# Seven block products for the second attention branch's queries, keys and values

## The reference, cut to what matters

```python
h = x @ w_in
qa, ka, va, qb, kb, vb = jnp.split(h, ...)
oa = windowed_gqa_sink(rope(qa), rope(ka), va, sink)
ob = neighborhood_attention(qb, kb, vb, rpb)
return jnp.concatenate([oa, ob], axis=-1) @ w_out
```

## Time and profile before

| | us |
|---|---|
| median of three runs (2304.95 to 2306.76) | 2305.78 |
| profiled execution, its own time | 2306.97 |
| its span | 2305.1 |
| TensorE busy in it (matmuls) | 2269.1 |
| VectorE, ScalarE, GpSimd busy | 979.0, 443.7, 73.8 |

### The profile page before, as it was taken

How to read it: one execution, slowest core, us unless ns; L and a number is a source line. 1 busy time by engine, 2 the same in 40 slices (tenths; PEclk the granted TensorE clock), 3 DMA queues, 4 the chain that set the end, 5 groups by cost and what they waited for, 6 DMA issues and landing times.

```text
span 2305.1 us, 25572 instructions
## 1 busy us (share of the span) xinstructions
PE 2269.1 (98%) x10790; PEld 1371.1 (59%) x10790; DVE 979.0 (42%) x1950; ACT 443.7 (19%) x1011; POOL 73.8 (3%) x130
## 2 busy tenths in 40 slices
PE   9999999999999999999999999999999999999998
PEld 6568547886487459997434433335999643333342
DVE  3567646667576557653211111125774311111122
ACT  3410003258110011220211211101132121111111
POOL 2000000000000000000000000000000000000000
PEclk9999999999999999999999999999999999999999
DMA  7279625354698415246999999995426599999997
GB/s 292 113 306 401 257 78 204 147 183 173 243 407 327 178 59 203 97 176 262 382 429 427 427 427 428 427 418 193 164 96 247 223 409 427 427 429 427 427 428 285
DMA packets 59168, 671.64 MB, mean 291 GB/s; under 512 B 7505, under 2 KB 7793, under 8 KB 18721
## 3 DMA queue, kind: packets, MB, share of 16 engines
q1 hardware_dynamic: 51888, 649.45, 69.1%
q0 software_dynamic: 7152, 20.43, 2.6%
HBM read 666.59 MB, written 3.26 MB: 291 GB/s over the span
## 4 chain that ended last, share of the span: by engine, by line
PE 87%; DMA 10%; DVE 3%; issue 0%; ACT 0%; SPq 0%; POOL 0%; DVEq 0%; POOLq 0%; ACTq 0%
PE ps L101 84%; DMA ring<-in_exp_w 8%; DVE arena L114 1%; PE ps L349 1%; DVE arena L117 1%; DMA arena<-ssm_rows 1%; PE ps L2753 1%; DMA ring<-in_ada_w 0%; PE ps L638 0%; DMA ring<-in_attn_w_in 0%; PE ps L1915 0%; DVE X L117 0%; PE ps L1234 0%; ACT arena L106 0%; DVE arena L110 0%
## 5 line engine op out<-in xcount | busy, mean ns | idle before, releaser
L101 PE MATMUL ps<-arena 128*64 128x512 f32 (+8 forms) x4036 | 954.6, 465 | 16.2 <-DMA arena<-in_exp_w 5.9
L101 PEld LDWEIGHTS ps<-arena 128*128 128x128 f32 (+2 forms) x4036 | 462.4, 167 | 464.5 <-issue 434.6
L101 PE MATMUL ps<-ring,arena 128*64 128x512 f32 (+2 forms) x1720 | 460.7, 584 | 3.2 <-DMA ring<-in_exp_w 3.2
L101 PE MATMUL ps<-XTGB,ring 128*128 128x256 f32 (+1 forms) x2160 | 423.5, 353 | 0.0
L101 PEld LDWEIGHTS ps<-XTGB,ring 128*128 128x128 f32 x2160 | 367.4, 191 | 52.5 <-issue 11.2
L101 PEld LDWEIGHTS ps<-ring,arena 128*64 128x64 f32 (+1 forms) x1720 | 174.9, 151 | 259.5 <-issue 253.9
L122 DVE COPY arena<-ps 128x512 f32<-128x512 f32 (+5 forms) x133 | 63.3, 496 | 417.4 <-PE ps L101 298.6
L121 ACT COPY arena<-ps 128x512 f32<-128x512 f32 (+3 forms) x179 | 81.5, 474 | 676.2 <-PE ps L2753 283.7
L101 PE MATMUL ps<-XTGB,arena 128*64 128x512 f32 (+2 forms) x736 | 200.7, 428 | 0.0
L105 ACT ACTIVATE arena<-ps 128x512 f32<-128x512 f32 (+2 forms) x95 | 51.2, 545 | 679.4 <-PE ps L101 674.6
L101 PE MATMUL ps<-ring,XTGB 128*128 128x512 f32 (+3 forms) x484 | 168.5, 503 | 2.9 <-DMA ring<-in_attn_w_in 2.7
(11 more groups left out here) (151 smaller groups left out, 949.8 us busy)
## 6 DMA issues: line engine op xcount, KB each, us to landing
arena<-in_exp_w SPq DMA_DIRECT2D x90, 2048.0 KB, 26.7
ring<-in_exp_w SPq DMA_DIRECT2D x68, 2048.0 KB, 27.9
ring<-in_mlp_w SPq DMA_DIRECT2D x25, 2048.0 KB, 8.8
ring<-in_ada_w SPq DMA_DIRECT2D x20, 2048.0 KB, 9.6
XTGB<-in_exp_w SPq DMA_DIRECT2D x18, 2048.0 KB, 32.3
ring<-in_ssm_w_in SPq DMA_DIRECT2D x12, 2048.0 KB, 7.6
ring<-in_w_in SPq DMA_DIRECT2D x12, 2048.0 KB, 7.8
ring<-in_gate_w SPq DMA_DIRECT2D x12, 2048.0 KB, 7.5
```

What stands on the lines that cost most here:

```text
L101: return self.e.matmul(o, lhsT=lhsT, rhs=rhs, start=start, stop=stop, skip_group_check=True)
```

## The change

q, k and v of the second branch are each made by seven block products. x's four block sums (`ab_x_sums`) are made once, on VectorE, after the first rope step. The weights' four block sums (`ab_sums`: three new blocks and one in place of a weight block, four instructions of 128x1024) are made on GpSimd for each of the three slabs. TensorE makes the products in four groups per slab (`ab_products`): group 0 the products 1 and 2 (added in PSUM), group 1 the products 6 and 5, group 2 the products 7 and 3, group 3 the product 4. For q and k a product is 2 x 4 matmuls over 128 columns, for v four over 256. ScalarE copies group 0's result (`ab_first`), VectorE adds the others (`ab_results`, seven adds per slab, after each pair's `normalise`). In the new `BETWEEN` the numbers 0 to 11 are 4 * slab + group, 12 to 15 are `out_a`, 16 is the first part of `out_b(0)`. The diff, cut to its core:

```diff
+        qX = [arena.get(4, P) for _ in range(4)]
+        qS = [[arena.get(4, T) for _ in range(2)] for _ in range(2)]
+        qS4 = arena.get(4, T)
-        BETWEEN = [((0,), (4,)), ((1,), (5,)), ((8,), ()), ((9,), ()), ((2,), (6,)), ((3,), (7,)), ((10,), (11,)),
-                   ((12,), (13,))]
+        BETWEEN = [((0,), (1,)), ((2,), (3,)), ((4,), (5,)), ((6,), (7, 8)), ((9,), (10,)), ((12,), (11,)),
+                   ((13,), (14,)), ((15,), (16,))]
+        AB_GROUPS = ((1, 2), (6, 5), (7, 3), (4,))
+
+        def ab_x_sums(v):
+            x1, x2, x3, x4 = qX
+            v.wait_ge(at("XT", 0, 0), at("XT", 0, 1))
+            k = v.then_inc(v.tt(x1, XT[:, 0:4, P:T], XT[:, 0:4, 0:P], ALU.subtract), "abX")
+            v.then_inc(v.tt(x3, XT[:, 4:8, P:T], XT[:, 0:4, P:T], ALU.subtract), "abX")
...
+        def ab_sums(e, k):
+            w = weights(f"ab{k}")
+            s1, s2 = qS[k % 2]
+            e.wait_ge(at("w", f"ab{k}"), at("abp", k - 2, 1) if k >= 2 else None)
+            i1 = e.then_inc(e.tt(s1, w[:, 0:4, T:2 * T], w[:, 4:8, T:2 * T], ALU.add), ("abS", k, 5))
+            e.wait_ge(i1)
+            i2 = e.then_inc(e.tt(s2, s1, w[:, 0:4, 0:T], ALU.subtract), ("abS", k, 6))
+            e.then_inc(e.tt(w[:, 0:4, T:2 * T], w[:, 0:4, 0:T], w[:, 0:4, T:2 * T], ALU.subtract), ("abS", k, 7))
+            e.wait_ge(i2, at("abp", k - 1, 2) if k else None)
+            e.then_inc(e.tt(qS4, w[:, 4:8, 0:T], s2, ALU.subtract), ("abS", k, 3))
...
+        def ab_products(pe, k, r):
...
+            ps = bank(pe, "abp", k, r, hold=r == 0)
+            pe.wait_ge(at("w", f"ab{k}"), at("abX"))
+            for n, p in enumerate(AB_GROUPS[r]):
+                x, y = pairs[p]
+                if p in (3, 5, 6, 7):
+                    pe.wait_ge(at("abS", k, p))
+                for f in range(1 if k == 2 else 2):
+                    for c in range(4):
+                        if k == 2:
+                            ins = pe.mm(ps[:, n * T:(n + 1) * T], x[:, c, :], y[:, c, :], c == 0, c == 3)
+                        else:
+                            ins = pe.mm(ps[:, n * T + f * P:n * T + (f + 1) * P], y[:, c, f * P:(f + 1) * P], x[:, c, :],
+                                        c == 0, c == 3)
+            pe.then_inc(ins, ("abp", k, r), *([("free", f"ab{k}")] if r == 3 else []))
+            if r == 1:
+                banks.drop(("abp", k, 0))
...
+        def ab_results(v, k, r):
+            c11, c12, c21, c22 = ab_parts(k)
+            def plus(o, q, n, x, *done):
+                return v.then_inc(v.tt(o, ab_product(k, q, n), x, ALU.add), ("read", "abp", k, q), *done)
+            v.wait_ge(at("abp", k, r))
+            if r == 1:
+                v.wait_ge(at("abP1", k))
+                e = plus(c12, 1, 0, c11, ("abU2", k))
+                v.wait_ge(e)
+                plus(c11, 0, 1, c11, ("ablow", k))
+            elif r == 2:
+                v.wait_ge(at("abU2", k))
+                e = plus(c21, 2, 0, c12, ("abU3", k))
+                f = plus(c12, 1, 1, c12)
+                v.wait_ge(e)
+                plus(c22, 1, 1, c21, ("abhigh", k))
+                v.wait_ge(f)
+                plus(c12, 2, 1, c12, ("ablow", k))
+            else:
+                v.wait_ge(at("abU3", k))
+                plus(c21, 3, 0, c21, ("abhigh", k))
...
         def attn_pool(pool):
             pool.stage("attn")
+            for k in range(3):
+                ab_sums(pool, k)
...
-                    pe.wait_ge(at("abT", i - 4), at("abT", i))
+                    part = "ablow" if i < 6 else "abhigh"
+                    pe.wait_ge(at(part, 0), at(part, 1))
...
-            out_b(0, (0, 1, 2))
+            out_b(0, (2,))
+            out_b(1, (0, 1))
             apply(AP - 1)
-            out_b(1, (0, 1, 2))
+            out_b(1, (2,))
...
                 for h in (2 * i, 2 * i + 1):
                     normalise(h)
+                for j in BETWEEN[i][0] + BETWEEN[i][1]:
+                    if j < 12 and j % 4:
+                        ab_results(v, j // 4, j % 4)
```

More of the change, by code:

```diff
@@ L538, in build @@
         abias = arena.get(8, 512)
+        qX = [arena.get(4, P) for _ in range(4)]
+        qS = [[arena.get(4, T) for _ in range(2)] for _ in range(2)]
+        qS4 = arena.get(4, T)
+        assert arena.pos <= BLOCK1
         AH, AP = 16, 8
-        BETWEEN = [((0,), (4,)), ((1,), (5,)), ((8,), ()), ((9,), ()), ((2,), (6,)), ((3,), (7,)), ((10,), (11,)),
-                   ((12,), (13,))]
+        BETWEEN = [((0,), (1,)), ((2,), (3,)), ((4,), (5,)), ((6,), (7, 8)), ((9,), (10,)), ((12,), (11,)),
+                   ((13,), (14,)), ((15,), (16,))]
@@ new lines, in build @@
+        AB_GROUPS = ((1, 2), (6, 5), (7, 3), (4,))
[4 more added lines that the diff above has]
+            v.then_inc(v.tt(x3, XT[:, 4:8, P:T], XT[:, 0:4, P:T], ALU.subtract), "abX")
+            v.wait_ge(k)
+            k = v.then_inc(v.tt(x2, XT[:, 4:8, P:T], x1, ALU.subtract), "abX")
+            v.wait_ge(k)
+            v.then_inc(v.tt(x4, XT[:, 4:8, 0:P], x2, ALU.subtract), "abX")
@@ new lines, in ab_product, with ab_parts @@
+        def ab_product(k, r, n):
+            ps = ps_of("abp", k, r)[:, n * T:(n + 1) * T]
+            return ps if k == 2 else ps.rearrange("p (f t) -> p f t", f=2)
+        def ab_parts(k):
+            if k == 2:
+                return vB[:, 0, 0:T], vB[:, 1, 0:T], vB[:, 0, T:2 * T], vB[:, 1, T:2 * T]
+            g = (qbT, kbT)[k]
+            return g[:, 0:2, 0:P], g[:, 0:2, P:T], g[:, 2:4, 0:P], g[:, 2:4, P:T]
+        def ab_products(pe, k, r):
+            w = weights(f"ab{k}")
+            s1, s2 = qS[k % 2]
+            x1, x2, x3, x4 = qX
+            pairs = {1: (XT[:, 0:4, 0:P], w[:, 0:4, 0:T]), 2: (XT[:, 4:8, 0:P], w[:, 4:8, 0:T]), 3: (XT[:, 4:8, P:T], qS4),
+                     4: (x4, w[:, 4:8, T:2 * T]), 5: (x1, s1), 6: (x2, s2), 7: (x3, w[:, 0:4, T:2 * T])}
+            ps = bank(pe, "abp", k, r, hold=r == 0)
[6 more added lines that the diff above has]
+                    for c in range(4):
+                        if k == 2:
+                            ins = pe.mm(ps[:, n * T:(n + 1) * T], x[:, c, :], y[:, c, :], c == 0, c == 3)
[5 more added lines that the diff above has]
+                banks.drop(("abp", k, 0))
@@ new lines, in ab_first @@
+        def ab_first(act, k):
+            act.wait_ge(at("abp", k, 0))
+            act.then_inc(act.cp(ab_parts(k)[0], ab_product(k, 0, 0)), ("abP1", k), ("read", "abp", k, 0))
+        def ab_results(v, k, r):
[19 more added lines that the diff above has]
+                plus(c21, 3, 0, c21, ("abhigh", k))
@@ L581, in attn_pe @@
                 turn(pe, ("akT",), t, lambda c: kdup[:, t, c * P:(c + 1) * P], 2, at("ak rope", t))
[L583 to L593, removed]
             def out_a(q):
@@ L643, in apply @@
                 ps = bank(pe, "av", i)
-                pe.wait_ge(at("avA" if i < 4 else "avB"))
+                pe.wait_ge(at("avA") if i < 4 else at("ablow" if i < 6 else "abhigh", 2))
                 for kc in range(2):
@@ L658, in between @@
                 for j in what:
-                    if j < 10:
-                        proj(j)
+                    if j < 12:
+                        ab_products(pe, j // 4, j % 4)
+                    elif j < 16:
+                        out_a(j - 12)
                     else:
-                        out_a(j - 10)
+                        out_b(0, (0, 1))
             for i in range(AP):
@@ L690, in attn_act @@
                 turned(act, ("aqT",), t, qT, 4, ("aqT",))
[L692 to L699, removed]
             def exps(h):
@@ L724, in between @@
                 for j in what:
-                    if j < 10:
-                        proj(j)
+                    if j < 12 and j % 4 == 0:
+                        ab_first(act, j // 4)
             for i in range(AP):
@@ L752, in attn_dve @@
                          rot_tmp, [("read", "aq", t)], [("aq rope", t)])
+                if t == 0:
+                    ab_x_sums(v)
             for t in range(2):
```

## The result

The changed kernel takes 2327.95 us (median of four runs, 2327.37 to 2328.24), the kernel before 2305.36 in the same sittings: ratio 1.0097, 95% interval 1.0084 to 1.0109, 22.6 us slower. The forecast was 9.6 us slower, and the range ended at 2320.5. The profiled execution's span grew from 2305.1 to 2326.4.

The account below looks back on a forecast made before the run. TensorE, busy for 98% of the span, was taken as the bound, so added waits count in full. Bank waits 5.4, sums 3.9 and 1.9, ropes' adds 0.8, less 2.4 of work: +9.6 on 2305.78, 2315.4 us; range 2308 to 2320.5.

Parts of the forecast that it names:

- bank waits: Before group 3 in pairs 1 and 3, TensorE waits for VectorE's adds to release group 1's bank: 2.7 us each, 5.4 together.
- sums in pair 1: GpSimd's sums hold up VectorE's multiplies of heads 2 and 3, so they start 3.9 us later, before the bank wait.
- sums in pair 3: A single GpSimd sum released in pair 3 delays VectorE's multiplies there by 1.9 us.
- ropes' adds: The ropes' last adds on VectorE wait for a GpSimd sum and delay scores(0): taken as 0.8 us.
- TensorE's work: Seven products save TensorE 2.4 us: q and k 28.5 instead of 29.5, v 12.9 instead of 14.3.
- slow clock: The prediction noted a granted clock of 1.00 in the head-pair loop and counted nothing for a slower clock after gaps.
- rival C: 128-column passes cost half a 256-column one (0.115 us) and VectorE is undisturbed: +0.3 us, 2306.1; chance 0.07.
- g: Time of one GpSimd sum of 128x1024: taken as 2.4 us, between 1.22 and 5.5.
- Rival B: GpSimd's sums are far slower, from 4 us up each: +15 to +20 us, 2321 to 2326; chance 0.10.
- A: Rival: bank wait alone, GpSimd's sums disturb nobody: +3.0 us, 2308.8; chance 0.25.
- GpSimd beside VectorE: In ropes and pairs 1 and 3, each wide VectorE pass waits for the GpSimd sum in flight: 0.8, 3.9, 1.9 us.
- Slower: The changed kernel is slower than the kernel before by over 4.6 us: chance 0.65.

Follow-up runs that it names:

- experiment 1: Changed kernel without GpSimd's twelve sums, plain weight blocks in their place (part of the computation left out): 2308.07 us, ratio 1.0011 to the kernel before.
- experiment 3: Changed kernel without GpSimd's sums (part of the computation left out) and with group 1's bank held until group 3 is issued: 2302.43 us, ratio 0.9984.
- experiment 2: Changed kernel with group 1's bank also held until group 3 is issued: 2317.01 us, ratio 1.0049 to the kernel before.
- experiment 7: Changed kernel with group 1's bank held, softmax multiplies on ScalarE, and GpSimd's sums begun after the last rope add: 2309.10 us, ratio 1.0016.
- experiment 4: Kernel before with twelve unread GpSimd additions of 128x1024 into scratch: 2332.53 us, ratio 1.0117.
- experiment 10: Kernel before with 24 back-to-back GpSimd memsets of 128x1024 into scratch: 2317.73 us, ratio 1.0054.
- experiment 6: Changed kernel with 38 and 14 unread matmuls filling TensorE's gaps ahead of group 3 of q and of k: 2328.21 us, ratio 1.0104.
- 8: Changed kernel with only the softmax's multiplies moved from VectorE to ScalarE: 2318.74 us, ratio 1.0056 to the kernel before.
- experiment 9: Changed kernel with all twelve weight sums on VectorE, group 1's bank held, k's group 0 moved to pair 1: 2301.63 us, ratio 0.9984.
- 5: Kernel before with twelve unread GpSimd additions, each waiting for the semaphore of the one before it: 2320.42 us, ratio 1.0067.

## Why the prediction was wrong

In the profiled executions the stage after attention begins 20.05 us later. Term by term (us):

| term | predicted | measured | from |
|---|---|---|---|
| bank waits | +5.4 | +5.0 | 2 x 2.50 in experiment 1 |
| sums in pair 1 | +3.9 | +7.3 | 9.80 - 2.50 |
| sums in pair 3 | +1.9 | +1.4 | 3.87 - 2.50 |
| ropes' adds | +0.8 | +4.7 | 38.75 - 34.08 |
| TensorE's work | -2.4 | -4.2 | experiment 3 |
| slow clock | 0 | +5.8 | below |
| after attention | 0 | +1.2 | 21.3 - 20.05, not a cost of the change |
| sum | +9.6 | +21.2 | span +21.3 |

The ropes' +4.7 holds 0.45 us that is not theirs: the main part of the input projection starts at 16.66 instead of 16.21, before any sum runs.

**TensorE's work** was mis-sized, and by more than its total says. The prediction had q and k save 1.0 us and v 1.4. From pass to pass q and k save 2.6 and v 1.6 (experiment 3). A pass of 128 columns costs 26.0/224 = 0.116 us there, not 0.127, which is rival C's price of 0.115. The 0.127 came from busy times, which hold a group's overlapping edges.

**The bank wait.** Right in place, size and releaser (7.7 - 5.1 is 2.6, where the prediction wrote 2.7; 2.50 was measured); holding the bank takes it away (2 against the changed kernel, 3 against 1).

**GpSimd's speed.** g = 2.4 was taken, 2.39 measured. Rival B (g of 4 and more) is out, although its 2321 to 2326 lay nearer to the result than the forecast. So is A. By the Trainium skill (GPSIMD Engine Reference, Elementwise — side-by-side cycle accounting) it was an estimate of 2.2; the trace is 0.2 above it.

**GpSimd beside VectorE.** This is the step that failed: not the direction, nor the sentence "each wide pass of VectorE waits for the GpSimd sum in flight", but the sum made from it. It lets head 2 wait g once and then do "its two multiplies", and head 3 once more: 2g - 0.95. In the trace each multiply waits for an addition of its own, since the next addition is running when the second multiply begins. That is four waits in pair 1. The four take 4.78 + 4.47 = 9.25 us instead of 1.23, and the 0.61 us that head 3 waited for ScalarE before goes: 7.4 us by this count, 7.3 measured, 3.9 predicted. The ropes' last adds, 0 to g in the prediction and taken as 0.8, are two passes and wait twice: 4.01 us instead of 0.49. In pair 3 a single addition runs, so only one multiply waits, and the single wait of the prediction came near (1.4 for 1.9). The range's upper end rested on the same count. Also wrong was "wide": passes of 128x2 are held as well. In the changed kernel those of the maximum lay, by chance, where GpSimd stood still between 41.98 and 55.13; experiment 7 moved the sums onto them.

The Trainium skill (SBUF — State Buffer, Who interferes with whom) says that the instruction issued first has the shared ports to its end and that the other is blocked until then. The runs agree on which passes are shut out: two SBUF inputs against reading additions but not against memsets, tensor_scalar against both, passes with a PSUM operand and reductions against neither, reciprocals not against additions. They agree on the length too, but for two passes. In experiment 4 an add that began 0.14 us before the first addition took 28.30 us beside twelve of them, and in experiment 10 a tensor_scalar took 10.85 beside memsets; there the measurement decides.

**Clock.** This is the term with the largest miss. The prediction noted the granted clock of 1.00, forecast gaps of 4.6 and 6.5 us, and put what they would do to the clock at nothing, without a reason. Against the same blocks at full clock in experiment 3: scores(0) 2.01 instead of 1.07, the first group 4.78 instead of 3.67, group 3 of q 3.57 instead of 1.89, the turns behind it 1.48 instead of 0.96, group 3 of k 3.39 instead of 1.89, together 5.8 us. Filling the gaps restored the last three (experiment 6).

**After attention** the 1.2 us are no cost of the change. The part behind attention takes 2177.4 us before and 2178.5 here, but 2175.6 in experiment 2, with the same code there, and 2176.6 to 2177.6 in the three experiments built on the kernel before. The clearest difference is a stretch of slow clock: from 1128.5 to 1132.0 us the changed kernel's granted clock is 0.50, while in experiment 2 it stays at 1.00 through that place, and TensorE passes it 1.6 us faster. Experiments 1, 3, 8 and 9 have the stretch, 2, 6 and 7 do not. Why is open.

**Chances.** "Slower" had 0.65; all the range's width was spent on g and on whether there is a disturbance, none on how many passes it hits, and none on the clock. The direction was right by its reasons. That the misses did not add up to more is partly luck: TensorE's work, worth 1.8 us more than was counted, stands against them.

## What to carry to other kernels

Work that moves to GpSimd is not free because GpSimd is idle: list which VectorE passes run beside it, and count one GpSimd instruction of waiting for every one with two SBUF operands and every tensor_scalar, small ones too, and not one for each group of them. Where they must overlap, a pause in GpSimd's queue can help (28.30 us against 3.16 for one add, experiments 4 and 5). Better, use VectorE's own idle time, as experiment 9 did for half the price per sum. When a result is read late, ask which rotating buffer its reader holds. And price a TensorE gap with the matmuls behind it: here 3.8 to 9.8 us of idle time cost 1.5 to 2.2 us more.

## What the runs showed of the hardware that was not expected

- Each held VectorE pass of the changed kernel is let in when the one addition in flight ends, also where the next addition follows directly. Passes of 128 and 256 columns are done 0.15 us after that end, and the next pass of its kind waits for the next addition.
- Two passes were held far longer. An add of 0.69 us took 28.30 beside twelve additions, a tensor_scalar of 128x2 took 10.85 beside memsets. Both had begun just before a GpSimd instruction (0.14 and 0.02 us) in a queue without pauses. With pauses of about 0.1 us between the additions the add took 3.16.
- A tensor_scalar of 128x2 is shut out like one of 128x256 (2.27 us in experiment 7), while a 128x512 pass with a PSUM operand runs at 0.69 beside an addition.
- The clock fell behind one idle stretch of 2.50 us and not behind another of 2.50 in the same execution (experiment 1), so the length of the gap alone did not decide it.
